# Five edits to a two-block fp32 network kernel on one core: order of high and low products, norms by token halves, decay rows, end of the z projections, S5 parameters

## Chip, cores and metric

The kernel runs on one core of a Trainium2 chip. The metric is the device time of one execution in microseconds (of the slowest core, here the only one), given as the median of several runs. A smaller number is better.

## What is computed

256 tokens of width 1024 pass through two blocks, all in fp32. Cut to what matters:

```python
def first_block(x, ...):
    h = x
    for i in range(2):                                  # DEPTH = 2 layers
        f = swiglu(rmsnorm(h, ffn1_pre_g[i]), ...)      # hidden width 2816
        h = h + 0.5 * rmsnorm(f, ffn1_post_g[i])
        m = mixer(rmsnorm(h, mix_pre_g[i]), ...)
        h = h + rmsnorm(m, mix_post_g[i])
        f = swiglu(rmsnorm(h, ffn2_pre_g[i]), ...)
        h = h + 0.5 * rmsnorm(f, ffn2_post_g[i])
    return h
# mixer, branch a: z and x,B,C projections, a causal convolution, a state-space scan in two
# chunks of 128 tokens (32 heads), then
    y = y * silu(z)
    yg = y.reshape(b, l, 4, 512)
    yg = yg * rsqrt(mean(yg * yg, axis=-1) + eps)       # norm in 4 groups, then w_branch_a
# mixer, branch b: an S5 scan (64 groups, 64 complex states) of u, gelu, w_glu, w_branch_b
# the two are gated, added and multiplied by w_out
def second_block(x, mem, ...):
    # layer 0: conv mixer + attention to mem -> w_o -> layer_norm -> dense FFN -> layer_norm
    # layer 1: block-sparse attention + mem  -> w_o -> layer_norm -> MoE, 8 experts, top 2 -> layer_norm
```

## The kernel before, in words

The kernel writes the five instruction streams by hand. Each engine has its own function with the whole program in order, and they meet at semaphores; `n.one` and `n.due` count at build time what each semaphore has been given and what a wait asks for, and the table PER says by how much each loop raises them. An engine executes its stream strictly in order, so whatever stands behind a wait waits too.

**Weights.** They come from HBM in chunks of 128 x 2048 into a ring of three slots. For each chunk SyncE starts a DMA into `raw`; ScalarE's `convert` (L1181) copies it to `w_hi`, rounded to fp32r; VectorE's `convert` (L1640) subtracts, `w_lo = raw - w_hi`, and raises weights_ready; TensorE makes its products and raises chunk_used, for which ScalarE's next `convert` into that slot waits. Activations are split in the same way: `x_hi` and `x_lo` (8 feature tiles of 256 tokens), `k_hi` and `k_lo` (4 tiles, for hidden values). Each product is made three times in fp32r into one PSUM bank (`product`): high weight by high value (L622), low weight by high value (L623), high weight by low value (L624). PSUM banks 0 to 3 collect long sums, banks 4 to 7 projections.

**FFN.** 11 steps of 256 hidden columns. A step has a gate chunk in slot 0, an up chunk in slot 1, a down chunk in slot 2; `col_tile` makes 128 output columns for 256 tokens from one of them, and `token_chunk` (L675) multiplies the hidden values by the down chunk, 512 columns at a time, by token half t and k tile kt. ScalarE and VectorE make the hidden values (`stage`, then `k_hi` and k_lo at L1693).

**A crossing** is what lies between the last product of one sublayer and the first of the next. VectorE's `post_norm` multiplies the sums by the gain (L1681, L1683), ScalarE squares and adds them up (L1197, `square_sum`) and takes a root (L1193, `root`), VectorE takes the reciprocal (L1657, `inverse_root`) and updates H (L1686), one instruction for each half of the tokens. Then comes `pre_norm`: the same without a gain, then H is scaled (L1663), TensorE transposes it (L684, `turn_stream`), ScalarE writes x_hi (L1215), VectorE x_lo (L1672), and TensorE's first product of each k pair waits for x_ready, which stands for x_lo. `warm` (L618) puts filler products on TensorE meanwhile. In block 2 `layer_norm` (L2089 to L2097, x_lo at L2083) has this place.

**Mixer.** TICKS is the written order of 33 projection chunks: 4 u, 1 dt, 8 gate, 12 x/B/C (each followed by a convolution, `taps`), 8 z. Beside them run the pieces of the S5 branch and of the scan. The log decays of 32 heads lie as rows in `dt_rows[:, 4, :]`; for each z chunk TensorE spreads four of them over 128 partitions with an fp32 product whose weight is a broadcast column of the identity (L804, `ssd_prepare`), ScalarE makes exponentials of them (L1357 to L1364, `ssd_decay`), and `ssd_output` uses those. `dt_tok` (L2005) is the copy by tokens that the inputs of the scan need. Behind z stand the norm in four groups (squares L1423, sums over features L696, root L1368, reciprocal L1957 in `stage_a`), then 8 chunks of branch a (`r_chunk`, whose inputs `stage_a` writes to k_hi and k_lo, two tiles for each), 12 chunks of branch b, 4 of w_out.

**S5 parameters.** During the first FFN of each layer VectorE, ScalarE and GpSimd build the S5 tables in pieces hung on FFN steps by number (the dictionaries given to `ffn`; `s5_rows_a`, `s5_rows_b` L1732 to L1752, and so on), and TensorE transposes them when step S5_ROWS_AT is over.

## Time and profile before

| | before |
|---|---|
| median of 3 runs | 3128.28 us (3121.72 to 3130.35) |
| the profiled execution | 3136.18 us |
| its span in the trace | 3134.4 us |
| mean granted TensorE clock | 0.979 of full speed |
| busy: VectorE, ScalarE, GpSimd | 70%, 55%, 7% |
| read from HBM | 616.81 MB |
| the chain of waits, by engine | TensorE 78%, VectorE 14% |

The profile is one execution; the median is over several, and the profiled one took 7.9 us longer than it. Busy time is summed over the whole span, and TensorE's share stands with the rows further down. The chain of waits goes back from the last instruction to what released each: a share of 78% says that for most of the time nothing but TensorE's own work sets the pace. The MoE stage runs from 2290 us to the end.

### The profile page before, as it was taken

The page shows a single profiled execution, that of the slowest core. Times are in us where ns is not written, and L with a number is a line of the kernel's source. Part 1 is how long each engine was busy: PE and PEld are TensorE (multiplying, and loading weights), DVE is VectorE, ACT ScalarE, POOL GpSimd, SP SyncE. Part 2 cuts the span into 40 slices and gives each one's busy share as a digit, 9 for nine tenths or more (in the row PEclk, how much of TensorE's full clock was granted, in tenths as well). Part 3 has the DMA queues.
Part 4 walks back from the last instruction along what each step waited for, and adds up shares of the span by engine and source line. Part 5 has one row for each costly group of instructions (what it writes and reads, how often), then busy time and mean ns, then how long its engine had stood idle before and what let it go on. Part 6 is the DMA issues. An engine that isn't in the chain of part 4 may idle for free.

```text
span 3134.4 us, 52666 instructions
## 1 busy us (share of the span) xinstructions
PE 2988.7 (95%) x20975; PEld 2672.7 (85%) x20975; DVE 2189.0 (70%) x2521; ACT 1716.8 (55%) x1982; POOL 211.7 (7%) x146
## 2 busy tenths in 40 slices
PE   8998999999989989999999999999899999999997
PEld 7988998989989989988889888998677877778776
DVE  5778965665556779857555555555568888889887
ACT  4446765334444467763344444443456676667665
POOL 0060213000000512040000000000000000000000
PEclk9999999999999999999999999999899999999999
DMA  8543342546546543523555554545099999999995
GB/s 237 168 151 114 120 142 75 170 149 194 185 144 201 161 115 110 156 99 122 168 187 180 169 175 132 176 161 189 1 305 365 328 344 349 327 327 342 351 326 198
DMA packets 488737, 619.92 MB, mean 198 GB/s; under 512 B 34689, under 2 KB 439059, under 8 KB 488595
## 3 DMA queue, kind: packets, MB, share of 16 engines
q1 hardware_dynamic: 488595, 617.91, 60.1%
q8 instruction: 104, 1.70, 0.2%
q14 instruction: 38, 0.31, 0.0%
HBM read 616.81 MB, written 1.05 MB: 197 GB/s over the span
## 4 chain that ended last, share of the span: by engine, by line
PE 78%; DVE 14%; ACT 4%; issue 3%; DVEq 0%; DMA 0%; SPq 0%; ACTq 0%
PE PS L1081 13%; PE PS L622 12%; PE PS L623 12%; PE PS L624 12%; PE PS L675 11%; DVE w_lo L1640 3%; PE PS L1106 3%; PE PS L1108 3%; PE PS L1107 3%; ACT w_hi L1181 1%; PE PS L1058 1%; ACT w_hi L1572 1%; PE PS L804 1%; PE PS L1116 1%; DVE act_out L1881 1%
## 5 line engine op out<-in xcount | busy, mean ns | idle before, releaser
L622 PE MATMUL PS<-x_hi,w_hi 128*128 128x256 f32 x3360 | 965.4, 287 | 14.0 <-DVE x_lo L2083 8.3
L623 PE MATMUL PS<-x_hi,w_lo 128*128 128x256 f32 x3360 | 956.7, 285 | 0.1
L624 PE MATMUL PS<-x_lo,w_hi 128*128 128x256 f32 x3360 | 956.2, 285 | 0.0
L1640 DVE TENSOR_TENSOR w_lo<-raw,w_hi 128x2048 fp32r<-128x2048 f32 x313 | 730.0, 2349 | 303.1 <-ACT w_hi L1181 302.4
L1181 ACT ACTIVATE w_hi<-raw 128x2048 fp32r<-128x2048 f32 x313 | 598.7, 1913 | 395.5 <-PE PS L675 246.8
L622 PEld LDWEIGHTS PS<-x_hi,w_hi 128*128 128x128 f32 x3360 | 651.1, 194 | 24.7 <-issue 13.3
L623 PEld LDWEIGHTS PS<-x_hi,w_lo 128*128 128x128 f32 x3360 | 651.3, 194 | 2.2 <-issue 0.3
L624 PEld LDWEIGHTS PS<-x_lo,w_hi 128*128 128x128 f32 x3360 | 650.7, 194 | 0.0
L1081 PE MATMUL PS<-w_hi,x_hi 128*128 128x512 f32 x704 | 284.7, 404 | 3.0 <-DVE stage L2277 2.3
L1081 PE MATMUL PS<-w_lo,x_hi 128*128 128x512 f32 x704 | 276.3, 393 | 0.0
L1081 PE MATMUL PS<-w_hi,x_lo 128*128 128x512 f32 x704 | 274.9, 391 | 0.0
L1705 DVE TENSOR_TENSOR k_hi<-act_out,PS 128x256 fp32r<-128x256 f32 x110 | 46.3, 421 | 292.7 <-PE PS L624 287.3
L2271 DVE TENSOR_TENSOR w_lo<-raw,w_hi 128x2048 fp32r<-128x2048 f32 x96 | 219.8, 2289 | 32.6 <-ACT w_hi L1572 32.4
L2271 DVE TENSOR_TENSOR w_lo<-XC,w_hi 128x2048 fp32r<-128x2048 f32 x88 | 201.7, 2292 | 33.9 <-ACT w_hi L1572 33.6
L1572 ACT ACTIVATE w_hi<-raw 128x2048 fp32r<-128x2048 f32 x96 | 183.8, 1915 | 15.5 <-PE PS L1108 14.0
L675 PE MATMUL PS<-w_hi,k_hi 128*128 128x512 f32 x568 | 179.2, 397 | 6.8 <-DVE k_lo L1976 5.4
L675 PE MATMUL PS<-w_lo,k_hi 128*128 128x512 f32 x568 | 176.8, 392 | 0.0
L675 PE MATMUL PS<-w_hi,k_lo 128*128 128x512 f32 x568 | 176.5, 392 | 0.0
L1235 ACT ACTIVATE act_out<-PS 128x256 f32<-128x256 f32 x55 | 21.1, 383 | 270.7 <-PE PS L624 270.7
L1572 ACT ACTIVATE w_hi<-XC 128x2048 fp32r<-128x2048 f32 x88 | 168.3, 1912 | 1.2 <-DMA XC<-in_w_gu_moe_dram 1.0
L1081 PEld LDWEIGHTS PS<-w_hi,x_hi 128*128 128x128 f32 x704 | 132.5, 188 | 31.2 <-issue 3.7
L1081 PEld LDWEIGHTS PS<-w_lo,x_hi 128*128 128x128 f32 x704 | 132.4, 188 | 29.6
(411 smaller groups left out, 4725.8 us busy)
## 6 DMA issues: line engine op xcount, KB each, us to landing
XC<-in_w_gu_moe_dram SPq DMA_DIRECT2D x176, 512.0 KB, 9.1
raw<-in_w_gu_moe_dram SPq DMA_DIRECT2D x132, 512.0 KB, 8.1
raw<-in_w_in_dram SPq DMA_DIRECT2D x64, 1024.0 KB, 5.7
raw<-in_ffn_w_gate_dram SPq DMA_DIRECT2D x44, 1024.0 KB, 5.4
raw<-in_ffn_w_up_dram SPq DMA_DIRECT2D x44, 1024.0 KB, 6.4
raw<-in_ffn_w_down_dram SPq DMA_DIRECT2D x44, 1024.0 KB, 5.0
raw<-in_w_down_moe_dram SPq DMA_DIRECT2D x32, 1024.0 KB, 10.2
G<-in_w_down_moe_dram SPq DMA_DIRECT2D x32, 1024.0 KB, 9.6
```

The lines of the kernel that those rows point to most:

```text
L622: mm(dst, w_hi[:, slot, w0:w0 + P], hi, start=start, stop=False, skip_group_check=True)
L623: mm(dst, w_lo[:, slot, w0:w0 + P], hi, start=False, stop=False, skip_group_check=True)
L624: return mm(dst, w_hi[:, slot, w0:w0 + P], lo, start=False, stop=True, skip_group_check=True)
L675: last = mm(PS[:, bank + 2 * t + b, :], left, right[:, slot, kt * D + 512 * b:kt * D + 512 * (b + 1)], start=False, stop=True, skip_group_ ...
L1081: last = mm(PS[:, 4, :], left, right, start=(k0 + k == 0 and right is whi and left is hi), stop=True, skip_group_check=True)
L1106: mm(PS[:, b, :], hi, whi, start=False, stop=True, skip_group_check=True)
L1107: mm(PS[:, b, :], lo, whi, start=False, stop=True, skip_group_check=True)
L1108: last = mm(PS[:, b, :], hi, wlo, start=False, stop=True, skip_group_check=True)
L1181: fn(w_hi[:, slot, :], raw[:, slot, :], ACT.Copy).then_inc(s["hi_ready"], n.one("hi_ready"))
L1572: fn(w_hi[:, MOE_SLOT[kind], :], MOE_RAW[kind][j % 3], ACT.Copy).then_inc(s["hi_ready"], n.one("hi_ready"))
L1640: tt(w_lo[:, slot, :], raw[:, slot, :], w_hi[:, slot, :].bitcast(F32), SUB)\
L2271: tt(w_lo[:, slot, :], MOE_RAW[kind][j % 3], w_hi[:, slot, :].bitcast(F32), SUB)\
```

## The change

The diff has five parts and some smaller edits.

1. **High parts first.** `first_tiles` makes the two products with x_hi of all its tiles first, and waits for xh_ready alone; the products with x_lo follow and wait for x_ready. It is used for the first FFN step of each FFN (both gate tiles), the first chunk of the mixer, of the memory block and of block 2's projections. The second of the converted slots moves behind x_lo.
2. **Norms by token halves.** `token_chunk` raises half_summed when the first half of the tokens is complete; `post_norm` and `layer_norm` then weight, square, take the root and update H one half at a time.
3. **Decay rows in one product.** The running sums are split into 32 rows of high and 32 rows of low parts in k_hi, the identity's columns stand twice in k_lo, and each head is one fp32r product with K = 64.
4. **The end of z.** Sums of groups 0 and 1 move ahead of the last `ssd_output`, that of group 2 ahead of branch a, that of group 3 behind its second chunk; squares 0 and 1 move into z chunks 5 and 6; reciprocals leave `stage_a`. The copy to dt_tok moves ahead of `taps`.
5. **S5 parameters.** S5_ROWS_AT becomes 3 and the pieces hang on earlier steps, `s5_rows_a` and `s5_rows_b` on the same one.

Besides: TensorE's layer loop is unrolled, `warm` goes from 16 to 12 products each, with new calls at the start and between the layers, and the first gate chunk is loaded alone.

```diff
@@ TensorE
+            def first_tiles(dsts, slot, width=256, banks=1, shared=False):
+                if shared:
+                    pe.wait_ge(s["x_ready"], n.due("x_ready"))
                 for k in range(DT):
+                    if k % 2 == 0:
+                        pe.wait_ge(s["xh_ready"], n.due("xh_ready"))
+                    for u, dst in enumerate(dsts):
+                        w0 = k * width + u * P
+                        mm(dst, w_hi[:, slot, w0:w0 + P], x_hi[:, k, :], start=(k == 0 and u < banks), stop=False,
+                           skip_group_check=True)
+                        mm(dst, w_lo[:, slot, w0:w0 + P], x_hi[:, k, :], start=False, stop=False, skip_group_check=True)
...
+                for k in range(DT):
+                    if k % 2 == 0 and not (shared and k == 0):
                         pe.wait_ge(s["x_ready"], n.due("x_ready"))
+                    ends = [mm(dst, w_hi[:, slot, k * width + u * P:k * width + (u + 1) * P], x_lo[:, k, :], start=False,
+                               stop=(k == DT - 1), skip_group_check=True) for u, dst in enumerate(dsts)]
...
+                        if kt == 1 and t == 0:
+                            last.then_inc(s["half_summed"], n.one("half_summed"))
...
-                              cst("ident", 32, 4 * i + h, 1).to_broadcast([32, P]), dt_rows[:, 4, :],
+                              head_pick[:, 4 * i + h:4 * i + h + 1].to_broadcast([64, P]), cum_both,
...
+                end_run(waiting=True)
+                def group_total(g):
+                    pe.wait_ge(s["group_sq"], n.due("group_sq"))
+                    if g >= 2:
+                        pe.wait_ge(s["group_root"], n.due("group_root"))
+                    sum_features(group_squares[g % 2], 4 + g % 2, 4).then_inc(s["group_sum"], n.one("group_sum"))
+                group_total(0)
+                group_total(1)
                 ssd_output(7)
-                warm(0, 5)
-                end_run()
...
-                for g in range(GROUPS):
-                    if g == 2:
-                        pe.wait_ge(s["y_ready"], n.due("y_ready", 2))
-                    pe.wait_ge(s["group_sq"], n.due("group_sq"))
-                    sum_features(group_squares[g % 2], 4 + g, 4).then_inc(s["group_sum"], n.one("group_sum"))
                 zero_acc()
+                group_total(2)
                 for i in range(8):
                     r_chunk(C_A + i, i)
+                    if i == 1:
+                        group_total(3)
...
-            with n.loop(pe, DEPTH, "layer"):
+            for l in range(DEPTH):
+                if l == 0:
+                    warm(4, 4)
...
-                warm(4, 16)
+                warm(4, 12)
...
+                if l + 1 < DEPTH:
+                    warm(4, 12)
@@ ScalarE
-                wait_used(pos[0] + 1)
-                square_sum(acc, 0, "squared")
-                act.wait_ge(s["weighed"], n.due("weighed"))
-                square_sum(acc, 1, "act_step")
-                root(3 if half else 0, (4.0 if half else 1.0) / D)
+                for t in range(2):
+                    act.wait_ge(s["weighed"], n.due("weighed"))
+                    square_sum(acc, t, "act_step")
+                    root(3 if half else 0, (4.0 if half else 1.0) / D, slice(t, t + 1))
...
+                    if kind == "z" and i in (5, 6):
+                        group_square(i - 5)
...
-                for g in range(GROUPS):
-                    if g >= 2:
-                        act.wait_ge(s["y_ready"], n.due("y_ready", 2 * g - 2))
-                        group_root(g - 2)
-                    fn(group_squares[g % 2], XC[:, 4 * g:4 * g + 4, :], ACT.Square)\
-                        .then_inc(s["group_sq"], n.one("group_sq"))
-                for g in (2, 3):
-                    group_root(g)
+                group_root(0)
+                group_root(1)
+                act.wait_ge(s["y_ready"], n.due("y_ready", 2))
+                group_square(2)
                 act.wait_ge(s["y5_done"], n.last("y5_done"))
                 for i in range(2):
                     fn(x_hi[:, 4 * i:4 * i + 4, :], U5[:, 4 * i:4 * i + 4, :], ACT.Copy)\
                         .then_inc(s["xh_ready"], n.one("xh_ready"))
+                act.wait_ge(s["y_ready"], n.due("y_ready", 4))
+                group_square(3)
+                group_root(2)
+                group_root(3)
                 for i in range(8):
                     convert((C_A + i) % RING)
...
-                ffn({3: (s5_exps,), 4: (s5_angles,), 6: (s5_tables,), 9: (lambda: s5_expand(0),)})
+                ffn({1: (s5_exps,), 2: (s5_angles,), 4: (s5_tables,), 9: (lambda: s5_expand(0),)})
@@ VectorE
+                dve.wait_ge(s["half_summed"], n.due("half_summed", chunks))
+                tt(weighted[:, 0, :], acc[:, 0, :], gain, MULT).then_inc(s["weighed"], n.one("weighed"))
+                wait_used(pos[0] + left)
                 tt(weighted[:, 1, :], acc[:, 1, :], gain, MULT).then_inc(s["weighed"], n.one("weighed"))
...
                 for t in range(2):
+                    inverse_root(slice(t, t + 1))
                     stt(H[:, t, :], weighted[:, t, :], sums[:, 1, t:t + 1], H[:, t, :], MULT, ADD)\
                         .then_inc(s["h_ready"], n.one("h_ready"))
...
-                step(RING - 1)
+                step(1)
...
+                for o in (0, 32):
+                    v.tensor_copy(head_pick[o:o + 32, :], con[o:o + 32, CONST["ident"][0] + o:CONST["ident"][0] + o + 32])
                 then(ins)
+                then(v.tensor_copy(cum_hi, cum))
+                tt(cum_lo, cum, cum_hi.bitcast(F32), SUB)
...
+                group_inverse(0)
                 ssd_outputs(7)
                 n.due("silu_conv", 2)
+                stage_a(0)
+                stage_a(1)
+                group_inverse(1)
+                low_parts(U5)
                 for i in range(8):
-                    if i == 0:
-                        stage_a(0)
-                        low_parts(U5)
-                    if i < 7:
+                    if 0 < i < 7:
                         stage_a(i + 1)
+                        if i in (2, 4):
+                            group_inverse(1 + i // 2)
                     convert((C_A + i) % RING)
...
-                pre_norm(0, (2,) if l else (0, 1, 2))
+                pre_norm(0, (1, 2) if l else (0, 1, 2))
                 pos[0] = -1
-                ffn({2: (s5_rows_a,), 3: (s5_rows_b,), 4: (s5_rows_c,), 5: (s5_columns, s5_turns), 6: (s5_powers,),
-                     7: (s5_projections,), 9: (lambda: v.memset(local, 0.0),)})
+                ffn({1: (s5_rows_a, s5_rows_b), 2: (s5_rows_c,), 3: (s5_columns, s5_turns), 4: (s5_powers,),
+                     5: (s5_projections,), 9: (lambda: v.memset(local, 0.0),)})
```

## Rows read from the trace of the kernel before

**Rows 1.** The page: busy time of each engine over the whole span.

```profile
PE 2988.7 (95%) x20975; PEld 2672.7 (85%) x20975; DVE 2189.0 (70%) x2521; ACT 1716.8 (55%) x1982; POOL 211.7 (7%) x146
```

**Rows 2.** The chain of waits, layer 0: start us, us, what.

```profile
715.47 5.47 PE PS L675 x24
```

**Rows 3.** Timeline of TensorE, first crossing: start us, us, instructions, [idle before <- releaser].

```profile
209.69 7.07 PE L618 MATMUL PS<-con 128*128 128x256 f32 x32
221.38 3.68 PE L684 MATMUL PS<-con,G 128*128 128x128 f32 x16 [4.62 <-DVE G L1663]
225.61 0.43 PE L622 MATMUL PS<-x_hi,w_hi 128*128 128x256 f32 x1 [0.56 <-DVE x_lo L1672]
```

**Rows 4.** Timeline of VectorE, first crossing.

```profile
205.71 6.52 DVE L1640 TENSOR_TENSOR w_lo<-raw,w_hi 128x2048 fp32r<-128x2048 f32 x2
...
215.07 3.75 DVE L1686 SCALAR_TENSOR_TENSOR H<-U,sums,H 128x1024 f32<-128x1024 f32 x2
```

**Rows 5.** Timeline of VectorE, crossing from mixer to second FFN, layer 0.

```profile
694.17 2.48 DVE L1686 SCALAR_TENSOR_TENSOR H<-U,sums,H 128x1024 f32<-128x1024 f32 x2
```

**Rows 6.** Timeline of TensorE, the same crossing.

```profile
699.20 1.97 PE L684 MATMUL PS<-con,G 128*128 128x128 f32 x16 [1.17 <-DVE G L1663]
702.35 0.39 PE L622 MATMUL PS<-x_hi,w_hi 128*128 128x256 f32 x1 [1.19 <-DVE x_lo L1672]
```

**Rows 7.** Windows: stretch, length, PE, PEld, DVE, ACT, POOL busy, granted clock, DMA share, GB/s.

```profile
219.00:226.00 7.00, 4.07 (x19) 3.67 (x20) 2.90 (x7) 3.49 (x10) 0.94 (x1) 0.52 0.00 0
...
895.00:908.00 13.00, 8.28 (x37) 7.88 (x38) 7.75 (x14) 8.92 (x16) 0.00 (x0) 0.50 0.61 202
1106.00:1117.00 11.00, 8.08 (x38) 7.68 (x39) 6.16 (x12) 6.69 (x14) 0.94 (x1) 0.53 0.01 1
```

**Rows 8.** Timeline of ScalarE, crossing from mixer to second FFN, layer 0.

```profile
700.55 3.02 ACT L1215 ACTIVATE x_hi<-PS,prm 128x256 fp32r<-128x256 f32 x8 [2.39 <-PE PS L684]
```

**Rows 9.** Timeline of TensorE, layer norm behind the dense FFN of block 2.

```profile
2116.99 0.36 PE L622 MATMUL PS<-x_hi,w_hi 128*128 128x256 f32 x1 [0.85 <-DVE x_lo L2083]
```

**Rows 10.** DMA issues, 0 to 40 us: size, median us from issue to landing.

```profile
con<-in_consts_dram SPq DMA_DIRECT2D x1, 581.5 KB, 6.1
```

**Rows 11.** Timeline of TensorE, start of the kernel.

```profile
16.70 0.58 PE L622 MATMUL PS<-x_hi,w_hi 128*128 128x256 f32 x1 [1.53 <-DVE x_lo L1672]
```

**Rows 12.** Timeline of TensorE, decay rows in the mixer, layer 0.

```profile
439.70 0.69 PE L798 MATMUL PS<-XC 128*128 128x256 f32 x2 [1.60 <-DVE dt_tok L2005]
...
440.55 3.59 PE L804 MATMUL PS<-rows,con 32*128 32x256 f32 x8
...
493.24 1.99 PE L804 MATMUL PS<-rows,con 32*128 32x256 f32 x8
```

**Rows 13.** Timeline of TensorE, start of branch a and its first hole.

```profile
537.18 0.39 PE L622 MATMUL PS<-k_hi,w_hi 128*128 128x256 f32 x1
...
550.62 0.39 PE L622 MATMUL PS<-k_hi,w_hi 128*128 128x256 f32 x1 [1.68 <-DVE k_lo L1693]
```

**Rows 14.** Timeline of ScalarE, last z projection and end of z, layer 0.

```profile
514.09 0.60 ACT L1408 ACTIVATE conv_out<-PS 128x512 f32<-128x512 f32 x1 [3.33 <-PE PS L624]
...
520.95 0.42 ACT L1364 ACTIVATE work<-work 128x256 f32<-128x256 f32 x1
...
529.73 1.28 ACT L1368 ACT_TABLE_LOAD   x1 [6.47 <-PE PS L696]
```

**Rows 15.** Waits of TensorE, whole span: us in total, times, longest us.

```profile
PE PS L747 <- DVE work L1875: 7.8, 2, 4.3
```

**Rows 16.** Timeline of VectorE, softplus and running sums, layer 0.

```profile
293.99 0.27 DVE L1924 TENSOR_SCALAR rows<-rows 32x128 f32<-32x128 f32 x1
```

**Rows 17.** Timeline of VectorE, end of z and branch a, layer 0.

```profile
531.53 1.75 DVE L1957 RECIPROCAL work<-work 128x256 f32<-128x256 f32 x1 [5.55 <-ACT work L1368]
...
545.24 2.29 DVE L1640 TENSOR_TENSOR w_lo<-raw,w_hi 128x2048 fp32r<-128x2048 f32 x1 [2.61 <-ACT w_hi L1181]
```

**Rows 18.** Timeline of TensorE, FFN step behind rows_b, layer 0.

```profile
100.09 0.74 PE L675 MATMUL PS<-w_hi,k_hi 128*128 128x512 f32 x2 [0.70 <-DVE k_lo L1693]
```

More of the change, by code:

```diff
@@ L221 @@
 S5_TILES = S5_PAIRS // 4
-S5_ROWS_AT = 5
+S5_ROWS_AT = 3
 S5_TABLE_AT = {4: 7, 6: 5, 8: 6}
@@ L355, in build @@
         dt_rows = rows[0:32]
+        cum_hi, cum_lo, cum_both = k_hi[0:32, 0, :], k_hi[32:64, 0, :], k_hi[0:64, 0, :]
+        head_pick = k_lo[0:64, 0, 0:32]
         s5row = flat(XC[0:32, 8:17, :]).rearrange("p (a n) -> p a n", n=P)
@@ L405, in load, with ffn_step @@
                   .then_inc(s[LANDED[slot]], 16)
-            def ffn_step(gate, up, down, at):
+            def ffn_step(gate, up, down, at, alone=False):
                 load(0, gate[:, bass.ds(at, 256)].rearrange("(k p) n -> p k n", p=P))
+                if alone:
+                    sp.wait_ge(s[LANDED[0]], 16)
                 load(1, up[:, bass.ds(at, 256)].rearrange("(k p) n -> p k n", p=P))
@@ L641, in c_chunk @@
                 pe.wait_ge(s["weights_ready"], n.due("weights_ready"))
-                for u in range(tiles):
-                    last = col_tile(PS[:, bank, u * T:(u + 1) * T], c % RING, u, width, fresh=fresh and u == 0)
+                if fresh:
+                    last = first_tiles([PS[:, bank, u * T:(u + 1) * T] for u in range(tiles)], c % RING, width, shared=fresh == "mem")[-1]
+                else:
+                    for u in range(tiles):
+                        last = col_tile(PS[:, bank, u * T:(u + 1) * T], c % RING, u, width)
                 last.then_inc(s["chunk_used"], n.one("chunk_used"))
@@ L710, in ffn, with first_step, step @@
             def ffn(rows=False):
-                def step(first=False, turned=False):
+                def first_step():
                     pe.wait_ge(s["weights_ready"], n.due("weights_ready"))
-                    col_tile(PS[:, 4, 0:T], 0, 0, fresh=first).then_inc(s["gate_a"], n.one("gate_a"))
-                    if first:
-                        zero_acc()
+                    gate_a, gate_b = first_tiles([PS[:, 4, 0:T], PS[:, 6, 0:T]], 0, banks=2)
+                    gate_a.then_inc(s["gate_a"], n.one("gate_a"))
+                    gate_b.then_inc(s["chunk_used"], n.one("chunk_used"))
+                    zero_acc()
+                    pe.wait_ge(s["weights_ready"], n.due("weights_ready"))
+                    col_tile(PS[:, 5, 0:T], 1, 0).then_inc(s["up_a"], n.one("up_a"))
+                    col_tile(PS[:, 7, 0:T], 1, 1).then_inc(s["chunk_used"], n.one("chunk_used"))
+                    token_chunk(2, 0)
+                def step(turned=False):
+                    pe.wait_ge(s["weights_ready"], n.due("weights_ready"))
+                    col_tile(PS[:, 4, 0:T], 0, 0).then_inc(s["gate_a"], n.one("gate_a"))
                     pe.wait_ge(s["weights_ready"], n.due("weights_ready"))
@@ L723, in step @@
                     token_chunk(2, 0)
-                step(first=True)
+                first_step()
                 if rows:
@@ L999, in _ @@
                 token_chunk(B_WO1 + i, i)
-            warm(4, 16)
+            warm(4, 12)
             turn_stream(H, "h_ready")
             ffn()
-            warm(4, 16)
+            warm(4, 12)
             turn_stream(H, "h_ready")
@@ L1029, in _ @@
                 token_chunk(B_WO2 + i, i)
-            warm(4, 16)
+            warm(4, 12)
             turn_stream(H, "h_ready")
@@ L1653, in low_parts, with inverse_root @@
                         .then_inc(s["x_ready"], n.one("x_ready"))
-            def inverse_root():
+            def inverse_root(t=slice(0, 2)):
                 dve.wait_ge(s["rooted"], n.due("rooted"))
-                then(v.reciprocal(sums[:, 1, :], sums[:, 1, :]))
+                then(v.reciprocal(sums[:, 1, t], sums[:, 1, t]))
             def pre_norm(g0, slots):
@@ L1997, in mixer @@
                         s5_table(S5_TABLE_AT[k])
+                    if k == 25:
+                        dve.wait_ge(s["dtok_psum"], n.due("dtok_psum"))
+                        v.tensor_copy(dt_tok[:, :, :].rearrange("p a h -> p (a h)"), PS[:, 3, 0:160])\
+                            .then_inc(s["dtok_ready"], n.one("dtok_ready"))
                     if 0 <= k - CONV_AT - 1 < 12:
@@ L2002, in mixer @@
                         s5_cvecs(t)
-                    if k == 25:
-                        dve.wait_ge(s["dtok_psum"], n.due("dtok_psum"))
-                        v.tensor_copy(dt_tok[:, :, :].rearrange("p a h -> p (a h)"), PS[:, 3, 0:160])\
-                            .then_inc(s["dtok_ready"], n.one("dtok_ready"))
                     if kind == "z":
@@ L2084, in split_stream, with layer_norm @@
                         .then_inc(s["x_ready"], n.one("x_ready"))
-            def layer_norm(src, split=True, late=None):
+            def layer_norm(src, chunks=0, left=1, split=True, late=()):
                 for t in range(2):
+                    if chunks and t == 0:
+                        dve.wait_ge(s["half_summed"], n.due("half_summed", chunks))
+                    if chunks and t == 1:
+                        wait_used(pos[0] + left)
                     then(stt(H[:, t, :], H[:, t, :], ALPHA, src[:, t, :], MULT, ADD, accum_out=sums[:, 0, t:t + 1]))
@@ L2100, in layer_norm @@
                     split_stream()
-                if late is not None:
-                    convert(late)
+                for slot in late:
+                    convert(slot)
             def attention(heads):
@@ L2131, in _ @@
             split_stream(4)
+            convert(1)
             convert(2)
```

59 lines of the change are left out of this document (30 added, 29 removed).

## The prediction

> **What bounds the kernel now.** I read the page first. TensorE is busy for 95% of the span [rows 1], so time comes off only where it stands idle, runs filler, or runs at the lower of its two clocks (granted 0.5, 1.2 GHz, against 1.0, 2.4 GHz). The chain of waits gives the pace of dense work: 24 products of 512 columns take 5.47 us, 0.228 us each [rows 2]. I then took the timeline engine by engine at the places that the diff touches.
>
> A crossing is the norm between two blocks. At the first (layer 0, FFN to mixer) the last product ends at 209.8 (F); then come 7.07 us of warm-up products, 4.62 us of idle time, the transposes at 221.38 and the first product at 225.61, F + 15.8 [rows 3]. VectorE is why: its two conversions run 6.52 us, to F + 2.4, and its two updates of H take 3.75 us [rows 4]. The mixer-to-FFN crossing has neither trouble: those updates take 2.48 us [rows 5], the transposes start at F + 8.1 (F is 691.1 there) and the first product at F + 11.3 [rows 6]. What differs is GpSimd: at the first crossing it is still building S5 tables, up to 0.94 us into the stretch from 219 [rows 7], and the change starts these two steps (34 us) sooner. In the stretch 219 to 226 the granted clock was 0.52, in 895 to 908 0.50 [rows 7].
>
> **Norms by halves and high parts first.** After the change only the second half's weighting, square, root, inverse and H update stand behind F; the first half runs from F - 1.4 (six products, 6 x 0.228). One update of 1.24 us [rows 5] leaves the chain, with its handover 1.3 us. Transposes: F + 6.8, behind the 12 warm-ups (12/16 of 7.07 = 5.3 us). The first product no longer waits for x_lo: ScalarE starts x_hi 1.35 us after the transposes start and makes eight in 3.02 [rows 8], so two are there at + 2.1 instead of + 3.15 at full clock [rows 6] or + 4.2 at half [rows 3]. The second conversion moved behind x_lo ends about 5.5 us after the first product and is needed at 5.8: nothing, but barely. The down weights follow 2.3 us later and have 11 us.
> - First crossing: 1.3 + 2.4 (conversion) + 1.3 (3.75 against 2.48) + 2.1 = 7.1 us. Its twin in layer 1 also ran its first products, from 1112.6 to 1116.9, at half clock [rows 7], 1.9 more: 9.0.
> - Layer 0 to 1: 1.3, less 0.7 because the parameter transposes now stand behind warm-ups, plus 2.2 and 2.6 for products that ran at half clock in 903 to 909 [rows 7]: 5.5.
> - Mixer to FFN, twice: 1.3 + 1.0 + 0.3 of stalls on x_lo = 2.6 each, 5.2.
> - Block 2: two layer norms, 1.5 for the half and 0.85 for the x_lo wait [rows 9], 4.6 together; router norm 1.5; memory block 1.5.
> - Kernel start: the constants land at about 7.4, 6.1 us after their issue [rows 10]. Four warm-ups at half clock (3.4 us) then push the parameter transposes from 9.2 to 10.9 and the root 1.7 us back; against it stand the x_lo wait of 1.53 [rows 11], an earlier gate load and an earlier full clock. I take +0.5, between -2 and +3.
>
> Sum 34.9 us.
>
> **Decay rows in one product.** Four heads are now 8 records in a pitch of 1.92 us [rows 12]. As fp32r each should run at the 0.12 us of the kernel's other 256-column products (96 in 11.76: 537.18 to 550.62 less the idle 1.68, [rows 13]): 0.48, saving 1.44. K grows from 32 to 64, which no row prices; bounds are 0.12 (a 128-row product) and 0.48 (today's pace); I take 0.12, since type and columns match. Of 16 groups the two last are covered by ScalarE (below), 13 give 1.44, and the first of layer 0 ran at half clock, 3.52 to 0.48: 21.8 us. Will others let it through? ScalarE idles 3.33 us per z chunk [rows 14], more than 1.44 + 0.5; the two squares put there (1.05 each) fit in two chunks, with about 0.5 us left. VectorE pays four small operations on the row that TensorE waits for (7.8 us over two waits, [rows 15]): at the 0.27 us of a small one [rows 16] that is 1.1 per layer (0.6 to 1.5), -2.2.
>
> The dt_tok copy ahead of the taps removes a 1.60 us wait in each layer [rows 12] and, in layer 0, most of what that dip in the clock cost the chunk behind it (1.7): 4.9 us.
>
> **The reordered end of z.** Count from the last tanh, Z = 514.1 [rows 14]. Branch a starts at 537.18, Z + 23.1 [rows 13]. New chain: decay(7) ends at Z + 7.3, table load 1.28, root 0.52 (531.53 less 529.73 and 1.28), reciprocal 1.75 [rows 14, 17] to Z + 10.9; gating of the last two tiles 1.8; first staging 1.34 (550.62 - 545.24 - 2.29 - 1.75, [rows 13, 17]): start at Z + 14.1, 9.0 us sooner. Group sums 0 to 2 and the last output fit ahead of it. In the loop the three holes of 1.68 [rows 13] go, 5.0 us, since the reciprocal no longer stands before staging. But **a new hole** opens. ScalarE now does root(3) before any of the eight conversions; root(3) needs sum 3, which TensorE makes only behind chunk 1; VectorE's convert(0) waits for ScalarE's, and stage_a(2) is queued behind it. So: chunks 0 and 1 to Z + 25.9, sum 3 (four fp32 products, priced like today's four heads at 1.9, [rows 12]) to 27.8, root 0.5, ScalarE conversion 1.9, VectorE's 2.29, staging 1.34: chunk 2 starts at 33.8, a hole of 6.0. It will probably pull the clock down: 2 us, bounds 0 and 3.4. A later reciprocal costs another 0.4. Net per layer 9.0 + 5.0 - 6.0 - 1.9 - 0.4 - 2.0 = 3.7; 7.4 for two.
>
> For the table load a page differs. The rows show 1.28 us of load and the root's reader 0.52 us behind it [rows 14, 17]. The Trainium skill (ScalarE: Activation LUTs, What ACT_TABLE_LOAD costs) adds a drain of about 1.4 us to each switch; by it the sum would be 2.8 us less. The trace decides.
>
> **Parameters two steps sooner.** rows_a and rows_b now run in one step, so rows_b waits for an exponential which waits for rows_a: about 1.0 us later in a step where TensorE already waits 0.70 [rows 18], so -2.0 for two layers. The GpSimd work falls on steps in which VectorE has slack; its gain is counted above. The unrolled layer loop costs nothing: its instructions are fetched beside running products; without that cover, a microsecond or two.
>
> **Sum.** 34.9 + 21.8 - 2.2 + 4.9 + 7.4 - 2.0 = 64.8 us. The profiled execution took 3136.2 us (span 3134.4), 7.9 above the median of 3128.3; nothing in the terms depends on that gap, so I take them off the median: 3063.5, rounded to 3063 us. The MoE stage, from 2290 on, is untouched.
>
> **Rivals.**
> - **No hole in branch a** (sum 3 turns out early enough, or I have a queue wrong). It gives back 2 x (6.0 + 2.0): 3047. For it: root(3) is one short instruction. Against: three in-order queues stand in the way. Chance 0.12.
> - **The clock dips at the crossings still.** Idle time of 1.6 us at 438 was followed by a stretch at 0.53, while two idle times of 1.17 and 1.19 at 699 to 702 [rows 6] were not. After the change each crossing has 1.5 us. If it dips at most of nine crossings, at 1.7 to 3 us each: 3082. Chance 0.20.
> - **The decay products don't get faster** (a broadcast weight column or K = 64 keeps them at 0.48 us): the change doesn't do there what it says, 3063 + 21.8 = 3085. For it: no row shows that form. Chance 0.08.
> - **Slower.** One mechanism, the granted clock: with fewer warm-ups every hole ends in a long stretch like 895 to 908, 13 us at 0.50, some 6.6 us each. Nine crossings, two holes in branch a and two ends of z are 13 places, 86 us: 3149. It decides from ten places on (65/6.6). Against it: of the holes in this trace only the longest, 8 us without any product, had such a stretch. Chance 0.03. The Trainium skill (TensorE: Matmul & The Clock Gate, What's actually happening) says that the low clock is the default and activity releases it, which speaks against shortening the warm-ups.
>
> The forecast itself has 0.55; 0.02 is left for no change. A difference of 0.3% (9.4 us) is about what a measurement of this kernel can tell from none. The forecast's unknowns (start, hole, clock, softplus row) make 3053 to 3072; reaching to the rivals on both sides gives 3043 to 3086. Faster 0.95, same 0.02, slower 0.03.
>
> **What would show each step.** First product after the first crossing at F + 8.9; L804's four heads at 0.5 us; no wait for dt_tok; branch a starting at Z + 14 and one hole of about 6 us behind chunk 1 in each layer, ended by k_lo; a wait of about 1.7 us in the step after rows_b; updates of H at 1.24 us each. I am wrong if the crossings keep their length, if ScalarE becomes late in z, or if the clock is lower on average than 0.979.

## The result, and the profile after

The changed kernel took 3088.72 us (median of 4, 3086.98 to 3091.12) against 3129.32 for the one before (median of 4); the ratio is 0.9868, with a 95% interval of 0.9852 to 0.9884. That is 40.6 us faster where 65.3 were forecast, and 2.7 us above the upper end of the range (3086). TensorE's row on the page answers to [rows 1]; the mean granted clock rose from 0.979 to 0.983.

```profile
PE 2946.3 (96%) x20867; PEld 2636.5 (85%) x20867; DVE 2191.1 (71%) x2535; ACT 1712.9 (56%) x1984; POOL 210.5 (7%) x146
```

TensorE's timeline gives the gain by stretches. F is the end of a stretch's last product, P the next first product; the spans went from 3134.4 to 3085.1 us, 49.3 us less.

| stretch | forecast gain, us | in the traces, us |
|---|---|---|
| start of the kernel (first product) | 0.5 | 16.70 to 16.20: 0.5 |
| second FFN step, layer 0 | 0 | -3.8 |
| crossing, first FFN to mixer, L0 / L1 | 7.1 / 7.1 | 15.8 to 9.25: 6.5 / 6.5 |
| mixer to second FFN, with stalls behind | 2 x 2.6 | 11.23 to 9.28, and 0.2: 2 x 2.15 |
| layer 0 to layer 1, with the FFN behind | 5.5 | 12.65 to 9.53, and 2.2: 5.3 |
| two layer norms | 4.6 | 2.0 + 2.2 |
| memory block | 1.5 | 2.0 |
| router norm | 1.5 | 0.0 |
| wait behind rows_b | -2.0 | 2 x -0.83 |
| both mixers up to z | -0.3 | 2.4 + 0.75 |
| z chunks, both layers | 26.7 | 6.0 + 4.5 |
| end of z to the end of the mixer, both | 7.4 | 5.9 + 1.5 |

The forecast column sums to 64.8 us. (The mixers' forecast before z is the softplus term of -2.2 and the 1.9 us of half clock behind the second crossing, which the forecast had in its 9.0.) The trace column sums to 44.9; the 4.4 us that are left lie in block 2 and MoE, in low-clock stretches and small pieces that no term claimed. They need no cause in the change: from the last FFN of block 1 on, the traces of this kernel and of eight experiments that change nothing there take from 1540.6 to 1545.0 us, and this one took 1541.1. **One row stands out: the z chunks, 10.5 for 26.7.** The second is the FFN step at 34 us. A third went the other way: the mixers up to z gained 3.2 us where 0.3 were to be lost. Waits of TensorE over the whole span (us in total, times, longest) name both:

```profile
PE PS L863 <- DVE XC L2009: 9.1, 12, 1.3
PE PS L626 <- DVE w_lo L1694: 4.1, 1, 4.1
PE PS L840 <- ACT work L1412: 3.6, 2, 1.8
```

L840 is the decay row product (L804 before), L863 the state product (L827 before). Before, no wait of the second and third kind shows, and those of the state product, 7.0 us in three, stood at the end of z (3.42 in each layer), not in the chunks.

**The z chunks.** TensorE's timeline in one even chunk, against [rows 12]:

```profile
493.82 0.72 PE L840 MATMUL PS<-k_hi,k_lo 64*128 64x256 f32 x4
494.47 0.66 PE L849 MATMUL PS<-con,XC 128*128 128x128 f32 x4
495.55 0.66 PE L863 MATMUL PS<-work 128*64 128x256 f32 x4 [0.42 <-DVE XC L2009]
```

The four heads now occupy 0.65 us from start to start of the next, where they took 1.92; K = 64 and the broadcast weight cost nothing that shows. But behind them TensorE waits, 0.42 us in even chunks and 1.06 in odd ones, for the outputs of the heads before (y_ready); the first two such waits of a layer are 0.36 and 1.34. VectorE's and ScalarE's timelines show why:

```profile
483.34 0.60 ACT L1460 ACTIVATE act_out<-PS 128x512 f32<-128x512 f32 x1 [2.71 <-PE PS L628]
...
483.97 0.69 DVE L2000 SCALAR_TENSOR_TENSOR act_out<-act_out,PS 128x512 f32<-128x512 f32 x1 [4.27 <-ACT act_out L1460]
484.57 0.48 DVE L2008 SCALAR_TENSOR_TENSOR XC<-XC,s5c,PS 128x256 f32<-128x256 f32 x1
485.08 0.43 DVE L2009 SCALAR_TENSOR_TENSOR XC<-XC,conv_out 128x256 f32<-128x256 f32 x1
...
485.56 0.66 PE L863 MATMUL PS<-work 128*64 128x256 f32 x4 [1.06 <-DVE XC L2009]
```

The z chunk's last product ends at 483.24; the tanh runs, VectorE gates z (L2000), and only behind that come the two instructions of the first output (L2008, L2009), although the state products that they read had ended at 477.3, and VectorE had been idle for 4.27 us. TensorE is ready for the outputs 1.3 us after the chunk's end (484.50) and gets them at 2.3. Before, the slow decay rows and the transposes filled 2.4 us there (472.63 to 475.06). The output that the state product needs was complete at 474.88, 0.2 us earlier, so TensorE never waited:

```profile
472.55 1.99 PE L804 MATMUL PS<-rows,con 32*128 32x256 f32 x8
...
474.46 0.42 DVE L1951 SCALAR_TENSOR_TENSOR XC<-XC,conv_out 128x256 f32<-128x256 f32 x1
...
475.06 0.71 PE L827 MATMUL PS<-work 128*64 128x256 f32 x4
```

**The dt_tok copy** did move ahead, and its wait of 1.60 us [rows 12] is gone. ScalarE's first group of exponentials is late in its place, by 1.82 us one z chunk later. The copy is no longer what holds it: it is made by 432.05, but ScalarE gets to the table load at 436.34, behind its own weight conversion, and the load and the exponentials take 6.3 us.

```profile
442.78 0.70 PE L840 MATMUL PS<-k_hi,k_lo 64*128 64x256 f32 x4 [1.82 <-ACT work L1412]
```

**The start.** SyncE's own timeline: the new wait for the first gate chunk holds the queue until 11.5 us, and the slow issue of an S5 load (6.41 us) stands behind it.

```profile
5.48 0.43 SPq L406 DMA_DIRECT2D raw<-in_ffn_w_gate_dram  x1
11.51 0.39 SPq L406 DMA_DIRECT2D raw<-in_ffn_w_up_dram  x1
...
16.55 6.41 SPq L463 DMA_DIRECT2D XC<-in_s_c_re_dram  x1
...
27.08 0.39 SPq L406 DMA_DIRECT2D raw<-in_ffn_w_gate_dram  x1
```

Before, the second step's gate load was issued sooner, at 24.05:

```profile
24.05 0.39 SPq L404 DMA_DIRECT2D raw<-in_ffn_w_gate_dram  x1
```

So TensorE stood idle ahead of the second FFN step, and ran its first products there at half clock:

```profile
38.67 0.58 PE L626 MATMUL PS<-x_hi,w_hi 128*128 128x256 f32 x1 [4.07 <-DVE w_lo L1694]
```

**The first crossing,** against [rows 3, 4]; F is 213.95. The first product came at F + 9.25 where F + 8.9 was named, the updates take 1.29 and 1.28, and nothing waits for x_lo:

```profile
215.63 1.29 DVE L1740 SCALAR_TENSOR_TENSOR H<-U,sums,H 128x1024 f32<-128x1024 f32 x1
217.03 1.28 DVE L1740 SCALAR_TENSOR_TENSOR H<-U,sums,H 128x1024 f32<-128x1024 f32 x1
...
220.87 1.97 PE L711 MATMUL PS<-con,G 128*128 128x128 f32 x16 [1.73 <-DVE G L1717]
223.20 0.35 PE L639 MATMUL PS<-x_hi,w_hi 128*128 128x256 f32 x1 [0.37 <-ACT x_hi L1264]
```

**Branch a.** The last tanh starts at 503.32 (Z), branch a at 517.42, Z + 14.1 as forecast, and the one hole of 6.03 us opens behind its second chunk, in both layers, through the ring that was named: root of group 3, weight conversion, k_lo.

```profile
530.93 0.47 ACT L1416 ACTIVATE work<-PS,eps 128x256 f32<-128x256 f32 x1 [13.46 <-PE PS L723]
531.30 3.70 ACT L1230 ACTIVATE w_hi<-raw 128x2048 fp32r<-128x2048 f32 x2
...
533.23 2.29 DVE L1694 TENSOR_TENSOR w_lo<-raw,w_hi 128x2048 fp32r<-128x2048 f32 x1 [8.15 <-ACT w_hi L1230]
...
536.92 0.55 PE L626 MATMUL PS<-k_hi,w_hi 128*128 128x256 f32 x1 [6.03 <-DVE k_lo L1747]
```

### The profile page after: what moved, and what is told of

Its sections match the earlier page's. It is cut to its first block, busy times and chain, and to the rows that moved or that the text cites. A ratio compares the mean times of both kernels' runs of the same rounds, so it can differ in the third digit from the quotient of the medians.

```text
span 3085.1 us, 52178 instructions
## 1 busy us (share of the span) xinstructions
PE 2946.3 (96%) x20867; PEld 2636.5 (85%) x20867; DVE 2191.1 (71%) x2535; ACT 1712.9 (56%) x1984; POOL 210.5 (7%) x146
## 3 DMA queue, kind: packets, MB, share of 16 engines
HBM read 616.81 MB, written 1.05 MB: 200 GB/s over the span
## 4 chain that ended last, share of the span: by engine, by line
PE 76%; DVE 15%; ACT 5%; issue 3%; DMA 1%; SPq 1%; DVEq 0%; ACTq 0%
PE PS L1130 13%; PE PS L626 12%; PE PS L628 11%; PE PS L627 11%; PE PS L700 11%; DVE w_lo L1694 3%; PE PS L1155 3%; PE PS L1157 3%; PE PS L1156 3%; ACT w_hi L1230 1%; ACT w_hi L1626 1%; PE PS L1165 1%; PE PS L1107 1%; DVE act_out L1935 1%; DVE work L1909 1%
## 5 line engine op out<-in xcount | busy, mean ns | idle before, releaser
L626 PE MATMUL PS<-x_hi,w_hi 128*128 128x256 f32 x3200 | 915.8, 286 | 4.1 <-DVE w_lo L1694 4.1
L627 PE MATMUL PS<-x_hi,w_lo 128*128 128x256 f32 x3200 | 909.1, 284 | 0.0
L628 PE MATMUL PS<-x_lo,w_hi 128*128 128x256 f32 x3200 | 908.6, 284 | 0.0
L626 PEld LDWEIGHTS PS<-x_hi,w_hi 128*128 128x128 f32 x3200 | 617.7, 193 | 12.3 <-DVE w_lo L1694 4.5
L627 PEld LDWEIGHTS PS<-x_hi,w_lo 128*128 128x128 f32 x3200 | 617.9, 193 | 1.9
L628 PEld LDWEIGHTS PS<-x_lo,w_hi 128*128 128x128 f32 x3200 | 617.6, 193 | 0.0
L1626 ACT ACTIVATE w_hi<-raw 128x2048 fp32r<-128x2048 f32 x96 | 183.7, 1914 | 16.8 <-PE PS L1157 14.1
## 6 DMA issues: line engine op xcount, KB each, us to landing
raw<-in_w_down_moe_dram SPq DMA_DIRECT2D x32, 1024.0 KB, 10.3
```

Of the source, the lines that this page charges most:

```text
L626: mm(dst, w_hi[:, slot, w0:w0 + P], hi, start=start, stop=False, skip_group_check=True)
L627: mm(dst, w_lo[:, slot, w0:w0 + P], hi, start=False, stop=False, skip_group_check=True)
L628: return mm(dst, w_hi[:, slot, w0:w0 + P], lo, start=False, stop=True, skip_group_check=True)
L1626: fn(w_hi[:, MOE_SLOT[kind], :], MOE_RAW[kind][j % 3], ACT.Copy).then_inc(s["hi_ready"], n.one("hi_ready"))
```

## The experiments

Each kernel is the changed one with the edit shown, unless it says otherwise.

**The kernel before once more.** The profiled execution was slower than the timed ones, and the forecast was taken off the median.

> The kernel before, unchanged, for a second trace. The first one took 3136.2 us where four other executions took 3121.7 to 3131.1. Theory A: the extra 5 to 8 us of that execution are low-clock stretches that come and go from run to run, above all the 13 us at a granted clock of 0.50 from 895 to 908 us and the 11 us at 0.53 behind 1106 us, which the prediction counted as recoverable; then this trace has a span of 3120 to 3130 us, the same instructions and waits, and those stretches are at full clock or shorter. Theory B: the two traces have the same dips in the same places, and the surplus is spread over the MoE stage (slower transfers); then the clock stretches agree within one or two.

It took 3133.48 us with a span of 3131.7. The low-clock stretches stand where they stood (895 us for 13.7, 1106 for 10.2, and nearly all of the some 20 others within a few us), so between these two executions the dips are the same ones. They differ by 2 us at the start, by 3 in the first mixer and by 2 in MoE.

That doesn't refute theory A, since this execution was nearly as long as the first. Over this study 25 executions of the kernel before took from 3117.9 to 3139.0 us, and each has its mean granted clock on record: the six shortest (up to 3121.9 us) had 0.985 or 0.986, the four longest (from 3135.6 us) 0.978 or 0.979. Going by those clocks, a short one has about 38 us less at half clock than the first trace has, which by estimate is worth at most 19 us; the times differ by 14 to 18. So the length of an execution goes with the time at half clock, as theory A had it, but both traces are of long executions, and which dips a short one lacks stays open.

**SyncE's wait.**

```diff
-                ffn_step(*ffn1, 0, alone=(l == 0))
+                ffn_step(*ffn1, 0)
```

> After, without the wait of SyncE for the first gate chunk (the load of up and everything behind it is issued at once, as in before). Theory A: that wait pushed SyncE's whole queue back by 3 us, so that the second FFN step stood idle for 4.07 us and ran its first products at half clock; without it the gap at 34.6 us goes, the first product comes about 0.5 us later, and the total falls by 4 to 6 us (about 3084). Rival: without the wait the gate chunk shares the DMA engines with the other two and lands late, and the first product moves back by as much as the gap gives; total within 1.5 us of after (3088.7).

3086.54 us, 2.2 less. The first product comes at 16.23, as late as with the wait (16.20): loading the gate chunk alone bought nothing. The gap is halved, to 2.00 us; the slow S5 issues still stand ahead of the second step's loads (the gate load goes out at 25.57). Mechanism right, size half. So the wait accounts for 2.2 of the 3.8 us in the table. The rest was there without it: the first step ends 2 us sooner than before (34.6 for 36.8), and the gate load of the second goes out 1.5 us later.

**Decay rows, undone.**

```diff
-                              head_pick[:, 4 * i + h:4 * i + h + 1].to_broadcast([64, P]), cum_both,
+                              cst("ident", 32, 4 * i + h, 1).to_broadcast([32, P]), dt_rows[:, 4, :],
```

> After, with the decay rows as fp32 products from the identity's column again (the extra copies of VectorE stay, and nobody reads them). Theory A: the faster rows only uncovered a wait of TensorE for VectorE's outputs of the heads before (y_ready), 1.06 us in odd and 0.42 us in even z chunks, so they are worth about 0.35 us per z chunk and some 2 us more at the first of each layer; this kernel is 6 to 10 us slower than after (about 3097) and has no waits on XC at the state products. Rival, the prediction's term: they are worth 1.44 us per group of four heads, 21.8 us together: 3110.

3093.39 us: the fast rows are worth 4.7 us in this kernel, not 21.8. With the slow rows no wait at a state product shows in the list, and the wait of L840 is 0.6 us where it was 1.8. Theory A holds, a little below its range.

**Outputs ahead of gating.**

```diff
-                        gate_z(i)
                         if i >= 2:
                             ssd_outputs(i - 2)
+                        gate_z(i)
```

> After, with VectorE's outputs of head pair i - 2 ahead of its gating of z chunk i, which waits for ScalarE's tanh and so for the end of z chunk i. Theory A: TensorE's wait in the z chunks is for those outputs alone; the waits of 1.34, 0.42, 1.06, 0.42, 1.06 us at the state products of each layer go, some 4 to 5 us per layer, 8 to 10 us together: about 3080. Rival 1: behind it GpSimd's masks or ScalarE's exponentials are as late, and only 0 to 3 us come off. Rival 2: VectorE's conversion of weights or the masks come later and TensorE waits there instead: no change or slower.

3077.53 us, 11.2 less. TensorE's waits at the state products fall from 9.1 us to this:

```profile
PE PS L863 <- DVE XC L2009: 0.4, 2, 0.2
```

Two z chunks take 18.0 us (458.01 to 476.05), where they took 20.0 after the change and 20.7 before it. A wait costs more than its idle time: where 1.06 us of it go, the next group of heads starts 1.29 us sooner (9.36 us after the last in place of 10.65). Between the traces the two mixers shorten by 9.4 us.

**Both.** The two edits together tell a hidden price from an additive one.

> After, with both edits of the last runs: VectorE's outputs ahead of its gating (alone: 3077.5 us) and the decay rows in fp32 again (alone: 3093.4). Theory A: the rows' price was hidden by the wait for the outputs and the other way round, so with the outputs out of the way each group of four heads costs its full 1.25 us more (1.92 against the 0.67 of the trace of after), 15 groups and the half-clock one, 18 to 20 us: 3096, no better than the decay rows in fp32 alone. Rival, additive effects: 3077.5 + 4.7 = 3082.

3093.92 us. With slow rows, moving the outputs changes nothing (3093.39 without it); with fast rows it brings 11.2. Or, read the other way: the fast rows bring 4.7 us behind the old order and 16.4 behind the new one. So the outputs' late place hid most of what the fast rows are worth, and the slow rows hid what the outputs' place costs.

**Root 3 later.**

```diff
                 group_root(2)
-                group_root(3)
                 for i in range(8):
                     convert((C_A + i) % RING)
+                    if i == 1:
+                        group_root(3)
```

> After, with ScalarE's root of group 3 behind the first two weight conversions of branch a instead of ahead of all eight. Theory A: the hole of 6.03 us behind the second chunk of branch a in each layer is the ring root 3, conversion, k_lo, and nothing else; both holes go and with them two low-clock stretches: 13 to 15 us, 3074. Rival 1: the next chunk waits for ScalarE or VectorE in its place (a hole of 1 to 3 us stays): 3077 to 3083. Rival 2: the reciprocal of group 3 becomes late, and the hole moves to chunk 6.

3070.81 us, 17.9 less. Neither hole is there, nor the 6.8 us of half clock behind each, nor a new wait; only the 0.43 us at chunk 4, for the reciprocal, stays. The mixers shorten by 7.7 and 10.3 us. The first is the hole and half of the 3.2 us of products that ran at half clock behind it.

**S5 pieces at their old steps.** The step numbers of `ffn`'s two dictionaries and S5_ROWS_AT as in before.

```diff
-S5_ROWS_AT = 3
+S5_ROWS_AT = 5
...
-                ffn({1: (s5_rows_a, s5_rows_b), 2: (s5_rows_c,), 3: (s5_columns, s5_turns), 4: (s5_powers,),
-                     5: (s5_projections,), 9: (lambda: v.memset(local, 0.0),)})
+                ffn({2: (s5_rows_a,), 3: (s5_rows_b,), 4: (s5_rows_c,), 5: (s5_columns, s5_turns), 6: (s5_powers,),
+                     7: (s5_projections,), 9: (lambda: v.memset(local, 0.0),)})
```

> After, with the S5 parameter pieces at their old steps (first transposes behind step 5, the two pieces of rows in two steps). The prediction's terms: the H updates at the crossings from the first FFN to the mixer go back from 1.24 to 1.9 us each, with GpSimd busy beside them, so those crossings grow from 9.25 by 1.3 us and the clock may fall there; the wait behind rows falls from 1.53 to 0.70 us in each layer. Net 0 to +4 us: about 3091. Rival: the sooner parameters bring nothing at the crossings, and this kernel is 1 to 2 us faster than after.

3094.99 us, 6.3 more. The waits behind rows are 0.70 us again, but the crossings take 11.0 and 12.1 us, not 9.25. GpSimd runs until 220.6, where after the change it ends at 190.4, and beside it VectorE's conversion takes 3.39 us instead of 2.29:

```profile
208.38 3.39 DVE L1694 TENSOR_TENSOR w_lo<-raw,w_hi 128x2048 fp32r<-128x2048 f32 x1
...
214.61 1.61 DVE L1740 SCALAR_TENSOR_TENSOR H<-U,sums,H 128x1024 f32<-128x1024 f32 x1
...
216.33 1.93 DVE L1740 SCALAR_TENSOR_TENSOR H<-U,sums,H 128x1024 f32<-128x1024 f32 x1
```

**High products that wait for x_lo too.**

```diff
                     if k % 2 == 0:
+                        pe.wait_ge(s["x_ready"], n.due("x_ready"))
                         pe.wait_ge(s["xh_ready"], n.due("xh_ready"))
```

(and the other waits for x_ready in `first_tiles` go).

> After, with the high products of the first tiles waiting for x_lo as well as x_hi, pair by pair: the order of products stays, the early start goes. The prediction's term: x_lo comes about 1.1 us behind x_hi at each crossing, so nine crossings (start included) start 1.0 to 1.2 us later and may stumble over the later pairs: 8 to 12 us slower, 3099. Rival: the first weights, converted before x_lo, are what the first product waits for, and less than 3 us is lost.

3095.54 us, 6.8 more; the crossings lengthen by 0.6 to 1.0 us each, the start by 1.3. The prediction's term was 1.05 us: right, a little high, and the total is below the 8 to 12 us that were expected.

**Halves that wait for the last product.**

```diff
                 dve.wait_ge(s["half_summed"], n.due("half_summed", chunks))
-                tt(weighted[:, 0, :], acc[:, 0, :], gain, MULT).then_inc(s["weighed"], n.one("weighed"))
                 wait_used(pos[0] + left)
+                tt(weighted[:, 0, :], acc[:, 0, :], gain, MULT).then_inc(s["weighed"], n.one("weighed"))
```

(in `layer_norm` alike).

> After, with the first half's weighting (and in block 2 its first sum) waiting for the last product of both halves; the rest of the halves' order stays. The prediction's term: the half that now starts 1.4 us ahead of the last product takes one update of 1.24 us off the chain; eight norms behind long sums (six, and two layer norms plus the router's) lengthen by about 1.2 us each: crossings of 10.4 in place of 9.25, the total 9 to 11 us slower, 3099. Rival: the warm-up products (5.3 us) and ScalarE's squares set the end anyway, less than 3 us.

3107.78 us, 19.1 more, twice what was expected. The norms start 1.4 us later, and the crossings of block 1 grow by 1.4 to 1.9, those of block 2 by 1.3 to 1.8: 13 us for eight. TensorE's idle time ahead of the transposes is now 3.1 us, and at four of the five crossings of block 1 the clock falls: sixteen transposes take 3.02 us instead of 1.97. At the fifth, between the layers, 3.26 us of idle time leave it at full (1.94 us). Low-clock stretches stand behind four crossings where after the change none did, and behind the router's norm 24 us of them for 10.

```profile
220.21 3.02 PE L711 MATMUL PS<-con,G 128*128 128x128 f32 x16 [3.12 <-DVE G L1717]
```

**No warm-ups at the crossings.** The calls of `warm` with 12 go, at eight crossings; their products are filler, and nothing reads them.

> After, without the twelve warm-up products at each crossing (those at the start stay). Theory A (the prediction's rival of the clock): TensorE then stands idle for 7 us at each of eight crossings, the granted clock falls to 0.5 at most of them, and the transposes (1.94 us at full clock, 3.68 at half) and the first products run at half clock: 3 to 6 us each, 24 to 48 us slower, up to 3130. Rival: the clock falls only at some of them, 10 us slower or less.

3105.28 us, 16.6 more. The clock falls at every crossing: idle for 6.91 us, then transposes at half clock, and a mean granted clock of 0.970 over the span. But a crossing lengthens only by 0.9 to 1.1 us, since its length is VectorE's and ScalarE's, and the rest is lost on the products behind it: of 22 us between the traces, 14 come from the last FFN of block 1 on.

```profile
219.95 3.40 PE L711 MATMUL PS<-con,G 128*128 128x128 f32 x16 [6.91 <-DVE G L1710]
```

**The three faster edits together.**

> After, with the three edits that were faster alone: no wait for the first gate chunk (-2.2 us), outputs ahead of gating (-11.2), root 3 behind two conversions (-17.9). They lie in different stretches, so theory A adds them: 3088.7 - 31.3 = 3057. Rival: the low clock or ScalarE's work behind z couples the last two, and 5 us or more are lost against the sum.

3056.99 us, 31.7 less where the sum is 31.3: they add.

**Two more.** SyncE's order, and S5 pieces one step sooner than before in place of two (ScalarE's dictionary and S5_ROWS_AT alike).

```diff
+                ffn_step(*ffn1, 256)
                 if l == 0:
                     load_params(0)
-                ffn(*ffn1, first=1)
+                ffn(*ffn1, first=2)
...
+                ffn({1: (s5_rows_a,), 2: (s5_rows_b,), 3: (s5_rows_c,), 4: (s5_columns, s5_turns), 5: (s5_powers,),
+                     6: (s5_projections,), 9: (lambda: v.memset(local, 0.0),)})
```

> The three edits, and two more: SyncE issues the first layer's S5 parameter loads behind the weights of the second FFN step instead of ahead of them, and the S5 pieces come one step sooner than in before instead of two, with the two pieces of rows in two steps again. Theory: the stall of 2.0 us at the second FFN step goes; the wait behind rows falls from 1.53 to 0.70 us in each layer; GpSimd's tables end about 6 us before the crossing, where they end 23 us before it in after, so the crossings stay at 9.25 us. 3 to 4 us below three_edits. Rival: GpSimd reaches into the crossing, which then takes 11 to 12 us as with the old steps.

3055.68 us, 1.3 below the three, within their spread (3054.86 to 3058.31 against 3056.03 to 3060.49). In the trace what was expected is there: no gap at the second step, 0.70 us behind rows, crossings of 9.25 us. But the gap was down to 0.51 us in the trace of the three already, and the two first FFNs are only 1.6 us shorter together. The span is 4.1 us shorter because the part from the last FFN of block 1 on is, which no edit touches. That these two edits bring anything is not shown. It is the lowest median: ratio to before 0.9774, interval 0.9748 to 0.9801.

## Why the prediction missed

- **Decay rows in one product: the step that failed.** The price of the product was right (0.12 us a head, the four in 0.65 against the 0.48 named). "Will others let it through?" was answered by ScalarE's idle time and by room for the squares. It was never asked of y_ready, the semaphore of the very next instruction of TensorE. That path (end of the z chunk, tanh, gating, the first output) takes 2.3 us and did not show as a wait, since the slow rows and the transposes took 2.4: the slack was 0.2 us. Measured: 4.7 us for 21.8. With that wait out of the way they are worth 16.4. Of the other 5.4, 2.5 us went into TensorE's wait for ScalarE's exponentials (L840: 3.6 us with fast rows, 1.1 with slow ones), and the term had counted the first group at half clock. The rule "what is late next" needs the other inputs of the instruction that moves forward, not only the producer of its own.
- **The dt_tok copy.** Of 4.9 us about 2 came. The waits of 1.60 are gone, but one group on the exponentials, for which the forecast named no wait, are late. With slow rows that wait is still 0.57 us in each layer, and this part is the copy's; the rest of the 1.82 is the fast rows'. The clock, which the forecast had at full there in layer 0, is at half from 444.5 to 447.9 us.
- **SyncE's wait.** The forecast counted "an earlier gate load" as a gain. It bought nothing (16.20 against 16.23). The queue behind the wait, named nowhere, cost 2.2 us, and that the sooner end of the first step would meet the loads of the second was not asked either: together 3.8 us. Here the rule is to count every load behind a waiting one.
- **Crossings.** Right nearly everywhere, to 0.6 us each, with the clock at 1.0 in them. The halves' share was undersized and others, since the sums fit, oversized: making both halves wait costs 19 us, of which 13 are direct, for a term of 1.3 us a crossing. (The items of layer 0 to 1 add up to 5.4, not 5.5.) The router's norm gave its 1.25 us at the transposes and lost them before MoE. The granted clock fell 10.7 us behind F instead of 13.8, under the router's products, and the first down chunk's load is issued as late after F as before (21.8 us).
- **End of z and branch a.** Z + 14.1, the hole of 6.03, the 0.4 at the reciprocal and the net of 7.4 us are as named. The whole hole with its clock is worth 17.9 us by the experiment, against the 16 that the rival without it had.
- **Softplus row.** The cost of 2.2 us doesn't show in any run: TensorE's waits there were 7.8 and 8.9 us in the two traces before, are 6.9 after (L783), and 6.4 to 9.2 in those of the experiments.
- **Parameters two steps sooner.** 1.7 for 2.0 us, and the cover for the crossings is shown: 6.3 us for the whole part.
- **The base.** The sum was taken off the median though every term came from one execution that was longer than it. Between traces the gain was 49.3 us, between medians 40.6; of a miss of some 25 us, 15.5 are terms (64.8 less 49.3) and 8.7 are this. The trace before was 6.9 us above the median of its kernel and the trace after 1.7 below its own. The forecast counted 6.7 us for products at half clock behind two crossings; whether the shorter executions had those dips at all is not known.
- **The rivals.** Of "the clock dips at the crossings still" nothing came; with the warm-ups gone it would have. "The decay products don't get faster" came near the measured total (3085) for a wrong reason: they did, and others didn't follow. Against "slower" stood that only the longest hole of the trace before had a long stretch at half clock behind it; [rows 7] shows a second, 11 us at 0.53 from 1106 on, with a hole of only 4.60 us in it.

For the table load: ScalarE's last exponential ended at 510.62, the load began at 510.63 and took 1.28, the root began at 511.93. The Trainium skill (ScalarE: Activation LUTs, What ACT_TABLE_LOAD costs) adds a drain of about 1.4 us; none shows here, and the start at Z + 14.1 leaves no room for one.

## To carry to other kernels

Before a busy stretch is shortened, list for the instruction behind it every semaphore that it waits for and when each is given: a wait of zero in the trace may have only tenths of a microsecond to spare. On an in-order engine, put work whose inputs are long ready ahead of work that waits for what has just ended; here that line exchange brought 11.2 us, and without it the faster product which called for it brought 4.7. A wait added on a load queue is paid by every load behind it. And take a forecast off the execution that its terms were read from.

## What the hardware showed that was not expected

- An fp32r product with a broadcast weight column and K = 64 goes at the pace of a full one of 256 columns; four take 0.65 us where four fp32 products with K = 32 took 1.92.
- GpSimd's tensor operations slow VectorE's fp32 operations beside them by a quarter to a half (a conversion 3.39 for 2.29 us, an update 1.61 to 1.93 for 1.28).
- Idle time of 1.7 to 1.9 us ahead of the transposes left the granted clock at full in all block 1 crossings after the change. With 3.1 us it fell at four crossings, but with 3.26 us not at the fifth; with 6.9 to 7.0 us it fell at all five.
- Two executions of the same kernel fall to half clock at nearly the same places. Yet over 25 of them the time goes with the mean granted clock: 0.985 or 0.986 in the six up to 3121.9 us, 0.978 or 0.979 in the four from 3135.6 us on.
